# In products with both halves of h, long and short matmuls alternate by input block

## The reference

```
def swiglu(h, w_gate_up, w_down):
    gu = h @ w_gate_up                  # (256, 1024) x (1024, 2 * 2816)
    g, u = split(gu, 2)
    return (silu(g) * u) @ w_down

for each layer:
    h = rms_norm(x, ...)                # layers 2 and 3: scaled and shifted by ada
    y = attention(h, w_qkv, w_o, ...)   # layer 1: the mixer, with two sigmoid gates h @ w
    x = x + rms_norm(y, ...)
    h = rms_norm(x, ...)
    x = x + rms_norm(swiglu(h, ...), ...)
```

## Time and profile before

| | us |
|---|---|
| median of 3 runs | 968.23 |
| profiled execution, first to last instruction (span) | 967.4 |
| PE busy | 957.9 |
| PEld busy | 834.2 |
| DVE busy | 735.6 |
| ACT busy | 535.3 |
| matmuls at L620, busy | 295.2 |
| matmuls at L622, busy | 169.6 |

### The profile page before, as it was taken

The page is one execution under the profiler, slowest core; times in us unless marked ns, Lnnn a source line. Parts: engine busy times, 40 slices in busy tenths (PEclk is TensorE's granted clock), DMA queues, the critical chain, the costliest instruction groups (busy, mean ns, idle before and its releaser), DMA issues.

```text
span 967.4 us, 13640 instructions
## 1 busy us (share of the span) xinstructions
PE 957.9 (99%) x5528; PEld 834.2 (86%) x5528; DVE 735.6 (76%) x1134; ACT 535.3 (55%) x830; POOL 37.2 (4%) x59
## 2 busy tenths in 40 slices
PE   9999999999999999999999999999999999999997
PEld 7999989888888887888888888888997788888886
DVE  7799877787778767988688878767886678666563
ACT  6645553564454556665565454646666675444451
POOL 3000000020000001000000000001000100000000
PEclk9999999999999999999999999999999999999999
DMA  9776688459977753777467676764743266558511
GB/s 369 306 286 262 261 309 314 178 200 211 390 300 297 286 202 132 270 269 266 185 250 299 241 298 254 288 231 134 237 153 117 81 230 244 223 182 319 174 44 44
DMA packets 33151, 225.65 MB, mean 233 GB/s; under 512 B 4058, under 2 KB 4341, under 8 KB 6720
## 3 DMA queue, kind: packets, MB, share of 16 engines
q1 hardware_dynamic: 30960, 219.43, 61.7%
q0 software_dynamic: 1696, 5.08, 1.8%
q10 hardware_dynamic: 432, 0.26, 0.1%
HBM read 223.49 MB, written 1.26 MB: 232 GB/s over the span
## 4 chain that ended last, share of the span: by engine, by line
PE 88%; DVE 7%; ACT 3%; POOL 1%; issue 1%; DMA 0%; DVEq 0%
PE psum L620 25%; PE psum L622 13%; PE psum L664 9%; PE psum L665 9%; PE psum L666 9%; PE psum L582 5%; PE psum L583 4%; PE psum L584 4%; DVE low L509 3%; ACT high L503 2%; PE psum L888 2%; PE psum L317 1%; PE psum L736 1%; PE psum L735 1%; PE psum L737 1%; PE psum L956 1%
## 5 line engine op out<-in xcount | busy, mean ns | idle before, releaser
L509 DVE TENSOR_TENSOR low<-raw,high 128x2048 fp32r<-128x2048 f32 (+1 forms) x160 | 361.0, 2274 | 98.1 <-ACT high L503 97.9
L503 ACT ACTIVATE high<-raw 128x2048 fp32r<-128x2048 f32 (+1 forms) x160 | 299.3, 1896 | 20.9 <-DMA raw<-in_gate_up 8.8
L620 PE MATMUL psum<-h_both,high 128*128 128x512 f32 x1176 | 295.2, 393 | 0.0
L620 PEld LDWEIGHTS psum<-h_both,high 128*128 128x128 f32 x1176 | 213.3, 189 | 40.1 <-issue 0.7
L622 PEld LDWEIGHTS psum<-h_both,low 128*128 128x128 f32 x1216 | 165.6, 190 | 11.5
L622 PE MATMUL psum<-h_both,low 128*128 128x256 f32 x1216 | 169.6, 282 | 0.0
L664 PE MATMUL psum<-high,y_hi 128*128 128x512 f32 x328 | 129.2, 394 | 0.5 <-DVE y_lo L978 0.5
L665 PE MATMUL psum<-low,y_hi 128*128 128x512 f32 x328 | 128.0, 390 | 0.0
L666 PE MATMUL psum<-high,y_lo 128*128 128x512 f32 x328 | 127.7, 389 | 0.0
L518 DVE CUSTOM_DVE_ANT_0 raw<-raw,c_row 128x1024 f32<-128x1024 f32 x96 | 113.4, 1218 | 2.7 <-DMA raw<-in_ada 2.7
L629 ACT ACTIVATE work_v<-psum 128x256 f32<-128x256 f32 x120 | 43.5, 375 | 112.6 <-PE psum L622 112.6
(11 more groups left out here) (183 smaller groups left out, 1045.7 us busy)
## 6 DMA issues: line engine op xcount, KB each, us to landing
raw<-in_gate_up SPq DMA_DIRECT2D x66, 1024.0 KB, 5.5
raw<-in_ada SPq DMA_DIRECT2D x48, 1024.0 KB, 4.8
raw<-in_down SPq DMA_DIRECT2D x33, 1024.0 KB, 4.8
raw<-in_mix SPq DMA_DIRECT2D x14, 1024.0 KB, 6.8
raw<-in_moba_qk SPq DMA_DIRECT2D x8, 1024.0 KB, 5.3
raw<-in_diff_qk SPq DMA_DIRECT2D x8, 1024.0 KB, 4.9
raw<-in_qk SPq DMA_DIRECT2D x4, 1024.0 KB, 15.2
raw<-in_branch SPq DMA_DIRECT2D x4, 1024.0 KB, 6.1
```

What stands on the lines that cost most here:

```text
L503: nc.scalar.activation(high[n % N_HI][:, s], raw[i % N_RAW][:, s], ACT.Copy).then_inc(*rounded.up(n if key is None else key))
L509: nc.vector.tensor_tensor(low[i % N_RAW][:, s], raw[i % N_RAW][:, s], high[n % N_HI][:, s].bitcast(F32), ALU.subtract).then_inc(*rest.up(key))
L620: nc.tensor.matmul(o[:, :], a, h_both[:, k, :, :], start=k == 0, stop=False)
```

## The change

The second loop over k in `pe_both` is gone, and its matmul stands inside the first. For every k, the matmul with `high` is now followed at once by the matmul with `low` of the same k. The operands, the PSUM columns written, the number of instructions and the waits are the same; the first matmul of a bank still starts the accumulation, the last one (`low`, k = 7) ends it and signals.

```diff
--- before.py
+++ after.py
@@ -618,7 +618,6 @@
                         nc.tensor.matmul(both[:, :, tile_of(1)], a, h_both[:, k, :, tile_of(1)], start=False, stop=False)
                     else:
                         nc.tensor.matmul(o[:, :], a, h_both[:, k, :, :], start=k == 0, stop=False)
-                for k in range(KC):
                     m = nc.tensor.matmul(o[:, 0:S], wl[:, k, j * P:(j + 1) * P], h_hi[:, k, :], start=False, stop=k == KC - 1)
                 m.then_inc(*slab.up((name, index, j), *((n, (name, index), *alias) if j else ())))
```

## The result

The changed kernel takes 974.2 us in the median of five runs (974.0 to 974.7), the kernel before 968.9 in five runs of the same session. The ratio is 1.0058, with a 95% interval of 1.0047 to 1.0069: slower by 0.6%, 5.3 us. Four more runs on another occasion (e10) gave 1.0059 (1.0045 to 1.0072).

A forecast was written before the change was run, and what follows sets the result against it. The prediction took TensorE's queue to bound the kernel (busy 957.9 of 967.4 us). Passages -2.6 and 0.3 lost again gave -2.3; 967.4 - 2.3 + 0.8 around the span = 965.9 us, range 962.0 to 972.0.

The forecast's parts named there:

- part 1: Matmuls of `pe_both`: none added or removed; 147 blocks change order, five begun blocks keep their price.
- part 2: Semaphore waits around the block: weights already awaited ahead of both loops, evacuation at the same distance; cost 0.
- part 3: Passages between long and short matmuls in 147 blocks: a pair costs 346.7 ns plus e, e = 0; sum -2.6 us.
- The bounds, -7 and +10: Limits in ns on a pair's cost over 346.7: short ones save 7, or long ones pay 10 and nothing returns.
- A: The forecast, chance 0.45: passage toll between long and short matmuls all but gone, e near 0, 965.9 us.
- the 24 blocks behind `pe_moving`: Blocks behind L666: cost 2.76 us now and lose their clean run of long matmuls, +0.3 us.
- the first long ones of the down products: 27 runs at L664 pay 27 ns each behind a block; behind a single short matmul perhaps less, -0.3 us.
- part 4: 16 blocks between 297.31 and 371.73 us: their 0.3 us gain returns as a longer PE wait at L317.
- C: Rival, chance 0.20: in all 1176 pairs every long matmul pays about 6 ns, short ones return nothing; 972.3 us.
- B: Rival, chance 0.25: toll depends on the mix, not the order; e stays 2 to 3 ns, no change, 968.2 us.
- D: Rival, chance 0.10: every short matmul behind a long one costs 113 ns, no long one pays; 962.6 to 957.0 us.

The follow-up runs named there:

- e10: The changed kernel unaltered, run again in another session against the kernel before: 974.6 us, ratio 1.0059.
- e1: Kernel before with each block reordered to two long matmuls, two short, four times over: 968.2 us, ratio 0.9993.
- e6: Matmul with `low` altered per network (512 columns; operand `high`; other bank columns), gate slabs alternating, up slabs in runs of eight: 1005.0 us, one run, not compared.
- e7: Twenty widths beside 512 columns, alternating in network one, runs of eight in two; ten orders of 256 and 512 in three: 983.3 us, one run, not compared.
- e8: Kernel before, runs of eight kept, with 264 columns in place of 256 in the matmul with `low`: 966.3 us, ratio 0.9975.

## Why the prediction was wrong

The forecast was 965.9, the time is 974.2. Step by step:

1. Instructions and order (part 1): right, 13640 instructions in both spans.
2. Waits (part 2): right. The table of waits is the same in both traces.
3. Passages (part 3): **here it failed.** I took e = 0 for a pair over the clean 346.7 ns; it is +6.7 in the timeline above. The bounds, -7 and +10, held it, though the dearest long ones, at 241 ns, lie above the 226.7 + 10 that I had taken as the most. The value was reached by supposing that the price of a matmul depends on the one ahead of it alone, so that the first distance behind a passage (233) and the first return (113) make a pair. The triples of the profile after show what is wrong with it: they contain 232 and 113, but also 241 with 120, so the state that sets the price outlives a pair. The block trace had said so, with a toll that lasted five or six long matmuls; the prediction named this as the point against A and gave it too little weight. The rhythm that I had forecast exists, but only in six of the 147 blocks (423.50 above). Two smaller terms were off as well: the 24 blocks behind `pe_moving` stood at 2.766 us and not 2.76, and the first long ones of the down products paid 26.5 ns a run more, where I had them pay less.
4. What is lost again (part 4): wrong, if small. PE's longest wait before L317 is 0.4 us in both traces, and the L317 at 372.36 us starts at 374.29 after the change, so the stretch in which the chain ran over DVE and ACT neither covered anything nor took it back. A chain that leaves an engine is no proof that this engine stood still.

Of the rivals, C had the right side, place and size (e = +6, 972.3), but not the cause. By it a short matmul throws the array back to the start of a passage, and then runs of two would have cost as much as single ones. They cost 1.8 ns a pair over the clean price (e1), single ones 6.7. That its size came near is luck: it had long ones pay 6 and short ones return nothing, and the triples have long ones pay 9.7 in the mean and short ones return 3. B is refuted by 6.7 ns a pair. So is, for this stream, the formula of "TensorE: Matmul & The Clock Gate", Back-to-back issue gap, in the Trainium skill, which takes the distance from the columns alone (the page gives it for isolated matmuls). With 13.3 ns in place of 2.5 it does fit runs of 512 (e6, first network) and of 256, but not runs of 264 or 384 (e7). D's cheap short matmul exists (113 ns) but is paid back by the long one that follows.

What is shown: the loss lies in the distances of matmuls of unequal length, and neither in waits, buffers, PSUM columns nor the clock. Its size depends on the lengths, by no monotone rule, on how they are grouped, and, since one order ran in two rhythms, on the state in which it was entered. What stays open: what in the array or its feed makes the toll, whether the weight loads have a part in it, and what puts six blocks of the changed kernel into the rhythm that pays nothing.

## What to carry to other kernels

Where TensorE is the bound and matmuls of two lengths share its queue, read the distances between starts, not the busy time: the same instructions in another order moved this kernel by 0.6%, without one wait. Runs of 16 and 16 were 0.15% better than runs of eight, but runs of two were as good as runs of eight and better than runs of four, so longer is not always better. Price a new interleaving by a trace of that very pattern in its place, since neither the first-order sum nor the number of changes foretold it. If the output bank has room, try a few columns more: 264 in place of 256 made the kernel 0.25% faster (e8, the fastest version here).

## What the runs showed that I had not expected

A run of matmuls of 264 columns starts every 120 ns, like one of 256. In the runs of eight of e7, distances stay near 112 ns for every width from 64 to 240 columns (the first of a run excepted), so below about 240 columns a matmul with a weight load of its own gets no cheaper. Alternating with one of 512, the pair stops near 340 ns: it is that at 96, 128, 160, 192 and 240 columns alike, and 343 at 64 and 224.
